# Expert rows added into the residual rows in DRAM instead of stored as pairs and summed at the end

## What is computed

```python
# x: residual rows after the mixer, (544, 1024)
t = rms_norm(x, norm_ffn_g)
# top expert group of 4, top 2 of its 4 experts -> two (expert, weight) pairs per token
combine = jnp.sum(jax.nn.one_hot(expert_id, N_EXPERTS) * top_w[..., None], axis=1)
y = 0
for e in range(16):
    hid = jax.nn.silu(t @ w_expert_gate[e]) * (t @ w_expert_up[e])
    y = y + combine[:, e:e + 1] * (hid @ w_expert_down[e])
x = x + y
y_out = rms_norm(x, final_norm_g)
```

## Time and profile before

| | us |
|---|---|
| runs | 952.3 median of 3 (951.32 to 953.8) |
| the profiled execution's own time | 952.17 |
| its span, first to last instruction | 950.3 |

### The profile page before, as it was taken

The page is one execution under the profiler, slowest core; times in us unless marked ns, Lnnn a source line. Parts: engine busy times, 40 slices in busy tenths (PEclk is TensorE's granted clock), DMA queues, the critical chain, the costliest instruction groups (busy, mean ns, idle before and its releaser), DMA issues.

```text
span 950.3 us, 15615 instructions
## 1 busy us (share of the span) xinstructions
PE 849.2 (89%) x5052; PEld 749.3 (79%) x5052; DVE 616.4 (65%) x1053; ACT 506.3 (53%) x910; POOL 69.3 (7%) x81
## 2 busy tenths in 40 slices
PE   4998999999999999989898996399999999999930
PEld 4998999888889888879897885377877777777730
DVE  6264224676676767476455223589899899989957
ACT  6224214455554454454623211277888788788844
POOL 0000000000000000000000000111112112112202
PEclk9999999999999999999999997599999999999975
DMA  8622133033023123150423806379999999999534
GB/s 245 151 89 74 42 89 95 1 97 95 20 76 95 41 60 96 37 162 5 133 90 117 304 35 233 119 254 359 358 362 350 362 360 363 366 354 361 196 105 190
DMA packets 154355, 164.97 MB, mean 174 GB/s; under 512 B 19645, under 2 KB 139069, under 8 KB 153770
## 3 DMA queue, kind: packets, MB, share of 16 engines
q1 hardware_dynamic: 148506, 152.68, 48.7%
q0 software_dynamic: 5520, 11.15, 3.1%
q10 hardware_dynamic: 288, 0.59, 0.2%
HBM read 155.93 MB, written 17.36 MB: 182 GB/s over the span
## 4 chain that ended last, share of the span: by engine, by line
PE 80%; DVE 9%; ACT 5%; DMA 3%; issue 3%; ACTq 0%; POOL 0%; POOLq 0%; DVEq 0%; SPq 0%
PE ps L1356 25%; PE ps L1358 23%; PE ps L1357 23%; PE ps L1495 2%; ACT E L744 2%; PE ps L1664 2%; PE ps L1504 1%; PE ps L1617 1%; DVE wl L939 1%; PE ps L1476 1%; ACT wh L708 1%; PE ps L1684 1%; DMA gb<-in_norm_mix_g 1%; DMA xg<-h_rows,idn 1%; DVE x L1335 1%
## 5 line engine op out<-in xcount | busy, mean ns | idle before, releaser
L1285 DVE TENSOR_TENSOR wl<-rawM,wh 128x1024 fp32r<-128x1024 f32 x192 | 227.6, 1222 | 21.1 <-ACT wh L857 19.7
L857 ACT ACTIVATE wh<-rawM 128x1024 fp32r<-128x1024 f32 x195 | 200.1, 1055 | 10.9 <-PE ps L1358 10.1
L1356 PE MATMUL ps<-hTh,wh 128*128 128x272 f32 x448 | 132.1, 295 | 8.1 <-ACT plh L696 3.0
L1358 PE MATMUL ps<-hTh,wl 128*128 128x272 f32 x448 | 130.7, 292 | 0.0
L1357 PE MATMUL ps<-hTl,wh 128*128 128x272 f32 x448 | 129.8, 290 | 0.0
L1356 PE MATMUL ps<-wh,hTh 128*128 128x384 f32 x320 | 116.3, 363 | 8.4 <-ACT qkv L721 6.8
L1356 PE MATMUL ps<-wh,xh 128*128 128x512 f32 x256 | 105.1, 411 | 3.4 <-DVE xl L1308 2.5
L1358 PE MATMUL ps<-wh,hTl 128*128 128x384 f32 x320 | 108.0, 337 | 0.0
L1357 PE MATMUL ps<-wl,hTh 128*128 128x384 f32 x320 | 107.8, 337 | 0.0
L1357 PE MATMUL ps<-wl,xh 128*128 128x512 f32 x256 | 102.0, 398 | 0.0
L1358 PE MATMUL ps<-wh,xl 128*128 128x512 f32 x256 | 101.9, 398 | 0.0
(11 more groups left out here) (255 smaller groups left out, 1599.1 us busy)
## 6 DMA issues: line engine op xcount, KB each, us to landing
rawM<-in_w_expert_gate SPq DMA_DIRECT2D x131, 256.0 KB, 5.2
rawM<-in_w_expert_up SPq DMA_DIRECT2D x131, 256.0 KB, 7.5
rawM<-in_w_expert_down SPq DMA_DIRECT2D x64, 512.0 KB, 8.0
rawA<-in_w_in SPq DMA_DIRECT2D x64, 192.0 KB, 3.0
rawA<-in_w_in SPq DMA_DIRECT2D x20, 512.0 KB, 5.5
rawA<-in_w_attn_branch SPq DMA_DIRECT2D x8, 512.0 KB, 4.6
rawA<-in_w_out SPq DMA_DIRECT2D x8, 512.0 KB, 4.3
fy<-expert_rows SPq DMA_DIRECT2D x4, 1024.0 KB, 9.0
```

Of the source, the lines that this page charges most:

```text
L857: nc.scalar.activation(wh[:, c % S, :], rawM[:, slot, :], ACT.Copy).then_inc(m_hi, 1)
L1285: V.tensor_tensor(wl[:, c % S, :], rawM[:, slot, :], wh[:, c % S, :].bitcast(F32), ALU.subtract).then_inc(m_lo, 1)
L1356: T.matmul(out, sh, mh_, start=start, stop=False, **kw)
L1358: return T.matmul(out, sl, mh_, start=False, stop=stop, **kw)
```

## The change

- A new DRAM tensor `acc_rows` takes the residual rows: SP writes `x` into it (5 DMAs, 2.23 MB) after the normed rows are done.
- The pair weights `wgt` are written to a DRAM table `wd`, 8 bytes a token, and POOL fetches for each item the weight of every slot (`weights`: index copy and an indirect DMA of 4 bytes a partition into `wsl`).
- ACT multiplies by that weight as it copies PSUM to `yb`.
- The scatter goes to `acc_rows` by token index, and *adds* in the DMA (`compute_op=ALU.add`). Two scatters can hit the same token, so each waits until the one before has landed.
- At the end `acc_rows` is loaded, one row per token (2.23 MB). The sums on DVE, and the splitting of the last product over ACT and POOL, are gone: DVE makes every tile's product in one instruction.

```diff
             sp.dma_start(gb[:], a["final_norm_g"].partition_broadcast(P)).then_inc(gb_in, 16)
+            for t in range(4):
+                sp.dma_start(acc_rows[t * P:(t + 1) * P], x[:, t, :]).then_inc(acc_in, 16)
+            sp.dma_start(acc_rows[SEQ:TOK], x[LAST:P, 4, :]).then_inc(acc_in, 16)
             for par in range(2):
                 sp.wait_ge(y_out[par], Y0[par])
             sp.wait_ge(h2_mm, NT)
             for s in (RM - 2, RM - 1):
                 moe_load(s, 1, s % 12)
+            sp.wait_ge(wgt_done, 1)
+            sp.dma_start(wd[0:2 * SEQ].rearrange("(t p k) o -> p t (k o)", p=P, k=2), wgt[:, 0:4, :],
+                         allow_slow_non_contiguous=True).then_inc(wd_out, 16)
+            sp.dma_start(wd[2 * SEQ:2 * TOK].rearrange("(p k) o -> p (k o)", k=2), wgt[LAST:P, 4, :],
+                         allow_slow_non_contiguous=True).then_inc(wd_out, 16)
...
-            pairs = yd.rearrange("(t k) d -> t k d", k=2)
             for t in range(4):
-                sp.dma_start(fy[:, t], pairs[P * t:P * (t + 1)]).then_inc(fy_in[t], 16)
+                sp.dma_start(fy[:, t], acc_rows[P * t:P * (t + 1)]).then_inc(fy_in[t], 16)
                 if t == 0:
-                    sp.dma_start(fy[LAST:P, 4], pairs[SEQ:TOK]).then_inc(fy_in[4], 16)
+                    sp.dma_start(fy[LAST:P, 4], acc_rows[SEQ:TOK]).then_inc(fy_in[4], 16)
...
+            for j, t in enumerate(FINAL):
                 dst, r = (o["y_prompt"][0, t * P:(t + 1) * P], slice(0, P)) if t < 4 else (o["y_sample"][0], slice(LAST, P))
+                sp.wait_ge(f_done, j + 1)
                 sp.dma_start(dst, ob[r, t, :]).then_inc(f_out, 16)
...
+            def weights(i, par):
+
+                pool.tensor_copy(idw[:, par:par + 1], ydi[:, bass.ds(i, 1)]).then_inc(w_ch, 1)
+                pool.wait_ge(w_ch, i + 1)
+                pool.sem_inc(p_go, 1)
+                pool.indirect_dma_start(wsl[:, par:par + 1], None, wd[:, :],
+                                        bass.IndirectOffsetOnAxis(ap=idw[:, par:par + 1], axis=0),
+                                        bounds_check=2 * TOK - 1, oob_is_err=False).then_inc(ws_in[par], 16)
 
-            def scatter(i, par):
+            def scatter(i, ip, par):
 
                 pool.wait_ge(y_ev, 2 * i + 3)
                 pool.sem_inc(p_go, 1)
-                pool.tensor_copy(ydn[:, par:par + 1], ydi[:, bass.ds(i, 1)]).then_inc(p_ch, 1)
-                pool.wait_ge(p_ch, 2 * i + 4)
+                pool.tensor_copy(ydn[:, par:par + 1], idi[:, bass.ds(i, 1)]).then_inc(s_ch, 1)
+                pool.wait_ge(s_ch, i + 1)
                 pool.sem_inc(p_go, 1)
-                pool.indirect_dma_start(yd[:, :], bass.IndirectOffsetOnAxis(ap=ydn[:, par:par + 1], axis=0),
-                                        yb[:, par, :], None, bounds_check=2 * TOK - 1, oob_is_err=False).then_inc(y_out[par], 16)
+                pool.wait_ge(y_out[1 - par], 16 * ip + Y0[1 - par] + 16 * par)
+                pool.sem_inc(p_go, 1)
+                pool.indirect_dma_start(acc_rows[:, :], bass.IndirectOffsetOnAxis(ap=ydn[:, par:par + 1], axis=0),
+                                        yb[:, par, :], None, bounds_check=TOK - 1, oob_is_err=False,
+                                        compute_op=ALU.add).then_inc(y_out[par], 16)
...
+            pool.memset(wsl[:], 0.0).then_inc(xg_clear, 1)
...
+            gather(0, 0)
+            gather(1, 1)
+            pool.wait_ge(wd_out, 32)
+            weights(0, 0)
+            weights(1, 1)
+            pool.wait_ge(acc_in, 16 * NT)
...
                     pool.wait_ge(xg_mm, i + 1)
                     pool.sem_inc(p_go, 1)
-                    gather(i + 2, par, 2 * i + 3)
-                    scatter(i, par)
+                    gather(i + 2, par)
+                    scatter(i, ip, par)
+                    weights(i + 2, par)
...
                 act.wait_ge(y_out[par], Y0[par] + 16 * ip)
+                act.wait_ge(ws_in[par], 16 * ip + 16)
                 for b in range(2):
-                    nc.scalar.activation(yb[:, par, 512 * b:512 * b + 512], ps[:, 5 + b, :], ACT.Copy).then_inc(y_ev, 1)
+                    nc.scalar.activation(yb[:, par, 512 * b:512 * b + 512], ps[:, 5 + b, :], ACT.Copy,
+                                         scale=wsl[:, par:par + 1]).then_inc(y_ev, 1)
...
             for j, t in enumerate(FINAL):
-                act.wait_ge(f_sum, j + 1)
-                root(every if t < 4 else slice(LAST, P), t, fsq[:, j % 2, :] if t < 4 else fsq[LAST:P, j % 2, :], f_rt)
-                if j in (1, 3):
-                    scaled(FINAL[j - 1])
-                if j == 3:
-                    scaled(FINAL[j])
+                r = every if t < 4 else slice(LAST, P)
+                act.wait_ge(fy_in[t], 16)
+                root(r, t, fsq[r, j % 2, :], f_rt, fy)
...
-            V.tensor_copy(wgt[:, :, 0], rt[:, 4, :])
-            V.tensor_tensor(wgt[:, :, 1], rt[:, 4, :], rt[:, 12, :], ALU.mult)
+            link(V.tensor_copy(wgt[:, :, 0], rt[:, 4, :]))
+            V.tensor_tensor(wgt[:, :, 1], rt[:, 4, :], rt[:, 12, :], ALU.mult).then_inc(wgt_done, 1)
...
+            for j, t in enumerate(FINAL):
+                r = slice(0 if t < 4 else LAST, P)
+                dve.wait_ge(f_rt, j + 1)
+                link(V.reciprocal(rsx[r, t:t + 1], rsx[r, t:t + 1]))
+                V.scalar_tensor_tensor(out=ob[r, t, :], in0=fy[r, t, :], scalar=rsx[r, t:t + 1], in1=gb[r],
+                                       op0=ALU.mult, op1=ALU.mult).then_inc(f_done, 1)
```

More of the change, by code:

```diff
@@ L153, in build @@
         idi = small("idi", [P, ROWS + 2], I32)
-        ydi = small("ydi", [P, ROWS], I32)
+        ydi = small("ydi", [P, ROWS + 2], I32)
         wr = small("wr", [P, KD, EG + EXPERTS])
@@ L157, in build @@
         idn = small("idn", [P, 2], I32)
-        ydn = small("ydn", [P, 2], I32)
+        ydn = at("ydn", 98 * K + 128, [P, 2], I32)
+        idw = at("idw", 98 * K, [P, 2], I32)
+        wsl = at("wsl", 98 * K + 64, [P, 2])
         over = small("over", [P, 1], I32)
@@ L279, in build @@
         m_raw = [sem(f"m_raw{i}") for i in range(RM)]
-        m_hi, m_lo, m_mm, p_ch, p_go, xg_mm, xg_hi, xg_lo = (sem(n) for n in (
-            "m_hi", "m_lo", "m_mm", "pool_chain", "pool_go", "xg_mm", "xg_hi", "xg_lo"))
+        m_hi, m_lo, m_mm, p_go, xg_mm, xg_hi, xg_lo = (sem(n) for n in (
+            "m_hi", "m_lo", "m_mm", "pool_go", "xg_mm", "xg_hi", "xg_lo"))
         si_done, hid_done, hid_mm, hid_hi, hid_lo, y_ev = (sem(n) for n in (
@@ L287, in build @@
         fy_in = [sem(f"fy_in{i}") for i in range(NT)]
-        f_out, f_sum, f_rt, f_inv, f_scaled, f_gained, f_done = (sem(n) for n in (
-            "f_out", "f_sum", "f_root", "f_inverse", "f_scaled", "f_gained", "f_done"))
+        f_out, f_rt, f_done = (sem(n) for n in ("f_out", "f_root", "f_done"))
+        acc_in, wgt_done, wd_out = sem("acc_in"), sem("wgt_done"), sem("wd_out")
+        ws_in = [sem(f"ws_in{i}") for i in range(2)]
+        g_ch, s_ch, w_ch = sem("gather_copy"), sem("scatter_copy"), sem("weight_copy")
         id_m = cst[:, C_ID:C_ID + P]
@@ L542, in _, with gather @@
         def _(pool):
-            def gather(i, par, copies):
-                pool.tensor_copy(idn[:, par:par + 1], idi[:, bass.ds(i, 1)]).then_inc(p_ch, 1)
-                pool.wait_ge(p_ch, copies)
+            def gather(i, par):
+                pool.tensor_copy(idn[:, par:par + 1], idi[:, bass.ds(i, 1)]).then_inc(g_ch, 1)
+                pool.wait_ge(g_ch, i + 1)
                 pool.sem_inc(p_go, 1)
@@ L589, in _ @@
                     pair(ip)
[L592 to L595, removed]
         @block.scalar
@@ L620, in split_to, with root @@
                     split[0] += 1
-            def root(rows, t, scratch, done):
+            def root(rows, t, scratch, done, src=x):
                 roots[0] += 1
-                nc.scalar.activation(scratch, x[rows, t, :], ACT.Square, accum_out=rsx[rows, t:t + 1]).then_inc(ach, 1)
+                nc.scalar.activation(scratch, src[rows, t, :], ACT.Square, accum_out=rsx[rows, t:t + 1]).then_inc(ach, 1)
                 act.wait_ge(ach, roots[0])
@@ L951, in _ @@
             V.memset(idi[:, ROWS:ROWS + 2], 0)
+            V.memset(ydi[:, ROWS:ROWS + 2], 0)
             dve.wait_ge(gb_in, 16)
@@ L1265, in _ @@
             link(V.tensor_scalar(lv[:], ps[:, 4, 0:ROWS], 0.5, cst[:, C_NONE:C_NONE + 1], ALU.is_lt, ALU.mult))
-            link(V.scalar_tensor_tensor(out=ydi[:], in0=ps[:, 4, 0:ROWS], scalar=-1.0, in1=lv[:], op0=ALU.add, op1=ALU.add))
-            V.tensor_scalar(idi[:, 0:ROWS], ydi[:], 1, None, ALU.logical_shift_right).then_inc(id_done, 1)
+            link(V.scalar_tensor_tensor(out=ydi[:, 0:ROWS], in0=ps[:, 4, 0:ROWS], scalar=-1.0, in1=lv[:], op0=ALU.add, op1=ALU.add))
+            V.tensor_scalar(idi[:, 0:ROWS], ydi[:, 0:ROWS], 1, None, ALU.logical_shift_right).then_inc(id_done, 1)
             dve.wait_ge(ge_done, 1)
@@ L1327, in _ @@
```

(22 more changed lines are left out.)

22 lines of the change are left out of this document (4 added, 18 removed).

## The result

The changed kernel takes 945.0 us (median of 7 runs, 944.5 to 947.96) against 951.7 for the kernel before beside it (7 runs, 950.06 to 953.8): a ratio of 0.9934 [0.9922, 0.9946]. It is faster, by 6.7 us where I had forecast some 13. The profiled execution took 945.17 us with a span of 943.2, where my sum gave 936.8. So 6.4 us are to be found.

A forecast was written before the change was run, and what follows sets the result against it. PE was taken to set the time, with DMA equally full and its lag hidden by the ring. A 13.5 us gain at the end, 0 at the beginning and in the loop, gave 939 us, range 935 to 960.

The forecast's parts named there:

- my sum: Whole kernel: span ending at 936.8 instead of 950.3 us, plus 1.87 us around it, 938.7, predicted as 939.
- The bound, the room and the ring: Expert loop: PE sets the time; loads lag 0.8 us per item, hidden by 24 slots, with 14 us left at item 15.
- The add's cost on the engines: Loop, per item: adding scatter costs twice a copy, +0.74 us, +0.8 with weights; 10.4 us of lag, no stall.
- rival B: Loop: add costs engines 2.5 to 3.8 times a copy, ring just runs dry; 945, range 942 to 949; chance 0.17.
- Two of the signs that I had named for a wrong prediction: Signs named: PE gaps in the loop, a scatter landing after over 18 us, or first gather later than 6.6 us.
- The small writes: Beginning, weight table writes on SP: about 1 us to issue both, at most 1 us cost, taken as 0.
- The hoped gain of the gather: Beginning: first gather, 6.63 us beside six loads against 3.92 us for the idle scatter, might win up to 2.7 us.
- The end: After item 15: scatter 5.45 us, first tile load 3.8, roots limiting, product 1.29, writing out 3.3; gain 13.5 us.
- The five writes of residual rows: Beginning, on SP: 2.23 MB, 6.2 us in nearly idle engines, ending near 602, before the first gather.
- ACT's two copies with a scale: Loop: 1.15 us for 1024 columns against 1.05 without scale, 0.1 us an item, hidden; 1.6 us in all if not.
- The rival from the latency of a row: Loop: 2 us HBM latency paid once per row, 8.5 us an item, a kernel near 1025 us; no separate chance.
- Rival E: End not shorter: adding scatter lands 6 us later on idle engines, 5 us over the copy; 944 us; chance 0.03.

The follow-up runs named there:

- plain_extra_plain: The changed kernel with a copying instead of adding scatter, plus a second copying scatter per item to an array nobody reads: 941.72 us, ratio 0.9884.
- plain_scatter: The changed kernel with the add taken out of the scatter, which then only copies rows by token index: 940.82 us, ratio 0.9872.
- the spread runs: Filled slots permuted over the partitions: changed kernel 0.9894, kernel before 0.9987, two copying scatters 939.35 us, changed kernel with table writes and first loop loads late 0.9833.

## Why the prediction was right and wrong

**The bound, the room and the ring: right.** The argument that loads fall behind, that the ring's lead hides it, and that the add is free until the lead is used up held in every kernel whose spacing was read, by one law. `plain_extra_plain` shows it best: 1.24 us more an item than `plain_scatter`, and 0.9 us in the median. The room was 16.4 us where I took 14, which was in my favour. One reading was loose: the 19.23 us of the kernel before takes in the first items, in which SP still waits for slots (28.8 us from 615 to 740 us); over the last seven items it is 19.12. The law compares like stretches and isn't touched.

**The add's cost on the engines: the step that failed.** "+0.74, because the engines move 360 GB/s with their requests overlapped": the factor of two over a copy was right, the size of a copy was not. I divided the queue's time by all 16 engines, as if an item's rows lay on them evenly. An indirect copy of rows in 68 neighbouring slots cost 1.3 us and not 0.74, and with the slots spread it cost less; that the neighbours sit on half of the engines is inferred from this. The term was 1.42 us an item with the fetch, not 0.8, so the lag was 18.5 us, not 10.4, and 2.1 us came out as stalls. With 14 us of room this would have been 4.5; a larger room mended half of the error. It is rival B's outcome (the ring just runs dry, 945) and its place, items 13 to 15; its price in microseconds, 1.1 to 2.1 us an item, holds the measured 1.4. Its reason, an add that costs the engines more than two copies, was not what happened. That its time of 945 was met is luck in part: it has 5.9 us of stalls in its sum, where 2.1 us came, with 2.1 at the first gather, 1.3 of a later start and 0.8 at the end. Two of the signs that I had named for a wrong prediction are there, gaps of PE in the loop and a first gather above 6.6 us.

**The small writes: the second step that failed.** I priced them at 1 us at most and took 0. They cost the first gather 2.1 us, all on the path. I had looked at what it costs to issue them, and not at what they do to the traffic behind them. The hoped gain of the gather (up to 2.7 us) comes only without them and without the loads beside it: 1.4 us (5.22), and 2.5 (4.17) with the slots spread as well.

**The end: 12.6 of 13.5 us.** From item 15's index copy to the end of the span it took 36.66 us before (913.64 to 950.3) and 24.06 after (919.14 to 943.2). The last scatter took 6.03 us, not 5.45: the add's extra over the copy is 2.8 us, since the copy of rows by token takes 3.27 rather than the 3.92 of the earlier trace rows. The first load took 4.39 us, not 3.8. The five roots (931.30 to 938.49) took 7.19 against the forecast 7.35, the product 1.28 with POOL idle as said, and the rest 3.0 after the last product against 3.3.

**Hidden, as said.** The five writes of residual rows filled 594 to 604 us (share 0.78) and cost nothing that a row shows. ACT's two copies with a scale take 1.26 us, against 1.08 without in the kernel before, 0.18 us an item where I had taken 0.1:

```profile
917.64 1.26 ACT L912 ACTIVATE yb<-ps,wsl 128x512 f32<-128x512 f32 x2
```

and PE's step is unchanged. POOL's second copy and DMA of each item, and its waits, made nobody late.

**The rival from the latency of a row** (some 1025 us) didn't come: the whole adding scatter of 68 rows costs 2.73 us an item in a full queue, not 8.5. The Trainium skill's figure of 2 us at high load (DMA: Bandwidth & Descriptors, section "Latency and other measured facts") is thus not paid once for each row here; the rows overlap. Rival E's price, 5 us over the copy with the engines idle, was 2.8.

**Open.** With the fetch the steps of the loop alternate, by 0.55 us in the first two (18.70 and 18.15) and by 0.1 to 0.2 us later; without it they are even, 18.41 to 18.46 up to the stalls. Their mean doesn't move, and I didn't follow it up. Which engine carried which row no view shows; the spread runs tell only that the place of the rows counts, and by how much.

## What to carry to other kernels

Don't price an indirect DMA by the mean of 16 engines: where only part of the partitions is in use, it can cost nearly twice that. If bulk loads wait behind it, try spreading the filled slots over the partitions. When the loop's loads run behind but hidden, compute the lead that is left in microseconds, and count each new transfer against it for every item; it costs nothing until the lead is gone, and everything after. Keep small-packet DRAM writes away from the moment at which a latency-bound transfer starts.

## What the runs showed of the hardware

- With 544 packets of 8 bytes to DRAM (one a token) under way, the traffic behind them stood until they had landed at about 610 us (at most 16 GB/s from 606.0, 0 GB/s from 608.5 to 610.0), and the gather issued beside them takes 8.72 us instead of 6.38. 544 packets of 512 bytes in the same place landed in 2.3 us and cost the gather nothing (6.40). The row of the latter's DMA issue (KB, us to landing):

```profile
dummy_rows<-cst SPq DMA_DIRECT2D x1, 256.0 KB, 2.3
```

- The add costs one more copy of the row, by the page's queue shares (0.17 us per 4 KB, a copied row 0.173) as in the full queue (1.32 us an item, a second copy 1.24 to 1.34); on idle engines the adding scatter lands in 6.03 us where the copy lands in 3.27.
- A DMA share of 1.0 isn't a ceiling. It adds up packet times, to 3.39 in one microsecond of small writes; and with the filled slots spread it rose from 1.01 to 1.07 and the rate from 335 to 355 GB/s, in the kernel before from 360 to 371 GB/s, though SP waits for slots there.
